# The first norm of a two-block network: TensorE computes the shifts, and products are interleaved with the normed tiles

## What is computed

```python
def modulate(h, shift, scale):
    return h * (1 + scale[:, None, :]) + shift[:, None, :]

def macaron_ffn(x, mod3, norm_pre, norm_post, w_gate, w_up, w_down):
    h = modulate(rms_norm(x, norm_pre), mod3[:, 0], mod3[:, 1])
    y = (jax.nn.silu(h @ w_gate) * (h @ w_up)) @ w_down
    return x + MACARON_WEIGHT * mod3[:, 2][:, None, :] * rms_norm(y, norm_post)

mod = (jax.nn.silu(c) @ ada_w[layer] + ada_b[layer]).reshape(b, N_MOD, D_MODEL)
mod_ctx = (jax.nn.silu(c_ctx) @ ada_w[layer] + ada_b[layer]).reshape(1, N_MOD, D_MODEL)
x = macaron_ffn(x, mod[:, 0:3], *ffn1)
ctx = macaron_ffn(ctx, mod_ctx[:, 0:3], *ffn1)
```

## Time and profile before

| | |
|---|---|
| median of three runs | 3566.09 us (3564.87 to 3566.77) |
| the profiled execution, its own time | 3565.38 us |
| its span, from first to last instruction | 3564.1 us |
| TensorE busy | 3456.8 us, 97% |
| VectorE, ScalarE, GpSimd busy | 46%, 40%, 34% |
| TensorE busy, 0 to 60 us | 31.2 us |
| granted TensorE clock, mean | 0.991 |
| chain that ended last | TensorE 87%, VectorE 6%, ScalarE 4% |

### The profile page before, as it was taken

The page is one execution under the profiler, slowest core; times in us unless marked ns, Lnnn a source line. Parts: engine busy times, 40 slices in busy tenths (PEclk is TensorE's granted clock), DMA queues, the critical chain, the costliest instruction groups (busy, mean ns, idle before and its releaser), DMA issues.

```text
span 3564.1 us, 44801 instructions
## 1 busy us (share of the span) xinstructions
PE 3456.8 (97%) x17264; PEld 2749.1 (77%) x17264; DVE 1653.8 (46%) x3091; ACT 1431.5 (40%) x2426; POOL 1225.3 (34%) x549
## 2 busy tenths in 40 slices
PE   6999999888999999999999999999999999999999
PEld 4888899776688887877776788887877776778887
DVE  7977466557420115655542333232855453234132
ACT  3223455554532223354443344343354453344242
POOL 2554200000044443434332444444434333334443
PEclk9999999999999999999999999999999999999999
DMA  8565365221123323222222222323322222223332
GB/s 316 192 225 192 125 189 165 71 84 54 48 89 89 101 89 103 84 71 89 83 77 82 84 89 92 99 92 110 100 76 84 78 74 89 83 83 97 98 94 85
DMA packets 118564, 376.42 MB, mean 106 GB/s; under 512 B 15440, under 2 KB 16336, under 8 KB 117968
## 3 DMA queue, kind: packets, MB, share of 16 engines
q1 hardware_dynamic: 115872, 367.88, 32.5%
q10 hardware_dynamic: 2480, 5.68, 0.5%
HBM read 359.86 MB, written 2.10 MB: 102 GB/s over the span
## 4 chain that ended last, share of the span: by engine, by line
PE 87%; DVE 6%; ACT 4%; issue 1%; DMA 1%; POOL 0%; SPq 0%; ACTq 0%; DVEq 0%; POOLq 0%
PE ps L1423 26%; PE ps L1425 25%; PE ps L1424 25%; PE ps L1683 2%; PE ps L1702 2%; ACT b L1765 1%; PE ps L1665 1%; PE ps L1466 1%; DVE b L2192 1%; PE ps L1661 1%; PE ps L1725 1%; PE ps L1736 1%; PE ps L1474 1%; DVE b L2355 1%; DVE b L2260 0%
## 5 line engine op out<-in xcount | busy, mean ns | idle before, releaser
L2682 POOL TENSOR_TENSOR b<-b,b 128x1024 fp32r<-128x1024 f32 (+1 forms) x501 | 1156.0, 2307 | 2268.9 <-ACT b L1765 2266.0
L1423 PE MATMUL ps<-b,b 128*128 128x512 f32 (+1 forms) x4720 | 1792.2, 380 | 48.2 <-DVE b L2192 15.4
L1425 PE MATMUL ps<-b,b 128*128 128x512 f32 (+1 forms) x4720 | 1754.0, 372 | 0.0
L1424 PE MATMUL ps<-b,b 128*128 128x512 f32 (+1 forms) x4720 | 1753.3, 371 | 0.0
L1423 PEld LDWEIGHTS ps<-b,b 128*128 128x128 f32 x4720 | 889.9, 189 | 278.0 <-issue 81.0
L1425 PEld LDWEIGHTS ps<-b,b 128*128 128x128 f32 x4720 | 890.2, 189 | 160.4
L1424 PEld LDWEIGHTS ps<-b,b 128*128 128x128 f32 x4720 | 891.0, 189 | 155.9 <-issue 5.8
L1765 ACT ACTIVATE b<-b 128x1024 fp32r<-128x1024 f32 (+2 forms) x622 | 607.1, 978 | 323.8 <-PE ps L1425 313.6
L2317 DVE CUSTOM_DVE_ANT_0 b<-b,b,b 128x1024 bf16<-128x1024 f32 x112 | 223.5, 1996 | 32.3 <-DMA b<-in_ada 21.4
L1826 ACT ACTIVATE b<-b 128x512 fp32r<-128x512 f32 (+1 forms) x110 | 64.8, 589 | 371.1 <-DVE b L2236 268.5
L2192 DVE TENSOR_TENSOR b<-b,b 128x1024 fp32r<-128x1024 f32 (+2 forms) x121 | 135.4, 1122 | 109.7 <-ACT b L1765 109.4
(11 more groups left out here) (236 smaller groups left out, 2406.6 us busy)
## 6 DMA issues: line engine op xcount, KB each, us to landing
b<-in_w SPq DMA_DIRECT2D x458, 512.0 KB, 3.5
b<-in_ada SPq DMA_DIRECT2D x88, 512.0 KB, 5.3
b<-in_w SPq DMA_DIRECT2D x80, 384.0 KB, 3.1
b<-in_w SPq DMA_DIRECT2D x80, 320.0 KB, 2.9
b<-b SPq DMA_DIRECT2D x176, 64.0 KB, 2.0
b<-in_const SPq DMA_DIRECT2D x24, 256.0 KB, 3.9
b<-in_x SPq DMA_DIRECT2D x2, 1024.0 KB, 12.0
out<-b SPq DMA_DIRECT2D x8, 256.0 KB, 2.0
```

Source lines behind the costliest of these rows:

```text
L1423: pe.matmul(out, a[0], b[0], start=first, stop=False)
L1424: pe.matmul(out, a[0], b[1], start=False, stop=False)
L1425: return pe.matmul(out, a[1], b[0], start=False, stop=last)
L2682: then(pool.tensor_tensor(wlo[j % NS][:, 0:nk * w], raw[j % NR][:, 0:nk * w], whi[j % NS][:, 0:nk * w].bitcast(F32), ALU.subtract), "lop", j)
```

## The change

- TensorE makes the eight shift tiles of the first norm: each by eight products of a 128x128 piece of `ada_w` with a two-column piece of the two vectors (c and c_ctx at once), and DVE adds the bias (a 128x2 instruction from PSUM, L2333 of the changed kernel). For these tiles the host lays `ada_w` out the other way round. The two vectors come in a small array of their own (`sc`, 128x16), silu on ACT.
- So DVE's `ada` instructions for these eight shifts go, and in ffn1 the eight for the context's shifts too: 96 such instructions stand where 112 did.
- The order of the head: the loads begin with `sc`, the first half of x, c, the second half; then w0, two modulation tiles, w1, two, w2, and the other twelve. The squares come first; `prime`, `factors(i)` (scale tile 2i, shift tile 2i+1, `gain1`), `pn` and the nine products with normed tile i-1 are written round by round. Six products that only keep TensorE at work stand behind the sum of squares.
- The last six triples of the three output tiles (k = 6 and 7) go tile by tile and no longer in turns.
- The second vector and modulation tiles 16 to 18 are loaded at `rest`, and the next weight chunks at the `prime` steps; the load of the context waits for the last shift tile.
- The weave's rate is 0.36 and its first steps are other ones.

```diff
-JOBS = ([(p, (0,)) for i in range(8) for p in (8 + i, i)] + [(p, (1,)) for p in range(16)] + [(p, (0, 1)) for p in range(16, 40)]
+JOBS = ([j for i in range(8) for j in ((8 + i, (0,)), (i, (0, 1)))] + [(p, (1,)) for p in range(8, 16)] + [(p, (0, 1)) for p in range(16, 40)]
         + [(p, (0,)) for p in range(40, 72)])
+BY_TENSOR = tuple(range(1, 16, 2))
...
-    S += [do("init")] + ada[:2] + squares(0) + ada[2:10] + [do("gain1", i=i) for i in range(5)] + norm[:1]
-    S += [do("sel"), do("prime", j=0)] + norm[1:3]
-    for i in range(3):
-        S += ada[10 + 2 * i:12 + 2 * i] + [do("gain1", i=5 + i)] + ([do("prime", j=1 + i)] if i < 2 else []) + norm[3 + i:4 + i]
-    S += norm[6:] + [do("rest"), do("silu2")]
-    S += weave(ffn(0, "ffn1", ("pn", 0), L, 2),
-               ada[16:32] + [do("gain", k=0)] + [x for a in ada[32:56] for x in (a, do("gap"))] + ada[56:]
-               + squares(1) + prenorm(1), 0.38)
+    def factors(i):
+        return ada[2 * i:2 * i + 2] + [do("gain1", i=i)]
+    main = weave(ffn(0, "ffn1", ("pn", 0), L, 2),
+                 [do("gap")] * 6 + ada[16:24] + [do("gain", k=0)] + [x for a in ada[24:48] for x in (a, do("gap"))] + ada[48:]
+                 + squares(1) + prenorm(1), 0.36)
+    done = max(i for i, s in enumerate(main) if s["kind"] == "mm" and s["t"]["i"] < 2 and s["t"]["name"] == "fg" and s["last"])
+    first, main = [s for s in main[:done + 1] if s["kind"] != "gap"], main[done + 1:]
+    end = [first[19 + x + 3 * y] for x in range(3) for y in range(2)]
+    S += [do("init")] + squares(0) + [do("prime", j=0)] + factors(0) + norm[:1] + idle(0, 6) + [do("sel")]
+    S += norm[1:2] + [do("prime", j=1)] + factors(1) + norm[2:3] + [do("prime", j=2)] + first[:4]
+    for i in range(2, 8):
+        S += factors(i) + norm[1 + i:2 + i] + (first[3 * i - 2:3 * i + 1] if i < 7 else [])
+    S += norm[9:] + [do("rest"), do("silu2")] + end + main
...
+            elif k == "ada" and st["x"] in BY_TENSOR:
+                x = st["x"]
+                at.wait_ge(*n("cb", 2))
+                at.wait_ge(*ada_sem(x))
+                b = bank_of(st["bank"])
+                for i in range(8):
+                    p = pe.matmul(b[:, 0:2], ada_slot(x)[:, 128 * i:128 * i + 128], sc[:, :, i], start=(i == 0), stop=(i == 7))
+                p.then_inc(up("pada", x), 1)
...
             elif k == "rest":
+                at.wait_ge(*n("ada", BY_TENSOR[-1]))
                 act.dma_start(CX[:, :, :], CT.rearrange("p (t n) -> p t n", t=8)).then_inc(s["d_cx"], 16)
...
+                if x in BY_TENSOR:
+                    at.wait_ge(*n("pada", x))
+                    dve.tensor_scalar(mod[:, p, :], PB[st["bank"]][:, 0:2], pv("ada_b", p), None, ALU.add).then_inc(
+                        up("ada", x), 1)
+                    continue
```

More of the change, by code:

```diff
@@ L382, in schedule @@
     norm = prenorm(0)
-    S += [do("init")] + ada[:2] + squares(0) + ada[2:10] + [do("gain1", i=i) for i in range(5)] + norm[:1]
-    S += [do("sel"), do("prime", j=0)] + norm[1:3]
-    for i in range(3):
-        S += ada[10 + 2 * i:12 + 2 * i] + [do("gain1", i=5 + i)] + ([do("prime", j=1 + i)] if i < 2 else []) + norm[3 + i:4 + i]
-    S += norm[6:] + [do("rest"), do("silu2")]
-    S += weave(ffn(0, "ffn1", ("pn", 0), L, 2),
-               ada[16:32] + [do("gain", k=0)] + [x for a in ada[32:56] for x in (a, do("gap"))] + ada[56:]
-               + squares(1) + prenorm(1), 0.38)
+    def factors(i):
[5 more added lines that the diff above has]
+    first, main = [s for s in main[:done + 1] if s["kind"] != "gap"], main[done + 1:]
+    assert len(first) == 25 and first[0]["kind"] == "begin" and all(s["kind"] == "mm" for s in first[1:])
+    end = [first[19 + x + 3 * y] for x in range(3) for y in range(2)]
[4 more added lines that the diff above has]
+    S += norm[9:] + [do("rest"), do("silu2")] + end + main
     S += [do("gain", k=k) for k in range(1, 8)]
@@ L685, in number @@
         if k == "init":
+            mark("cb", 2)
             mark("cb", 0)
@@ L790, in number @@
         elif k == "ada":
+            if s["x"] in BY_TENSOR:
+                s["bank"] = brief()
+                mark("pada", s["x"])
             mark("ada", s["x"])
@@ L1173, in program @@
              "d_blk", "d_strip", "d_dh0", "d_dh1", "d_dh2", "d_dh3", "d_out"] + [f"d_raw{i}" for i in range(NR)]
[L1174 removed]
+            + [f"d_ada{i}" for i in range(15)] + [f"d_ring{i}" for i in range(4)] + ["d_cb0", "d_cb1", "d_sc"])
     s = {k: ctx.enter_context(nc.semaphore(k)) for k in list(SIGNALS) + DMAS + ["dve_own"]}
@@ L1319, in sp_program @@
             if k == "init":
+                sp.dma_start(sc[:, :, :], CB[:, 2048:2064].rearrange("p (v k) -> p v k", v=2)).then_inc(s["d_sc"], 16)
+                xt_ = XT.rearrange("p (t n) -> p t n", t=8)
+                sp.dma_start(X[:, 0:4, :], xt_[:, 0:4, :]).then_inc(s["d_x0"], 16)
                 sp.dma_start(cb[:, 0, :], CB[:, 0:1024]).then_inc(s["d_cb0"], 16)
-                xt_ = XT.rearrange("p (t n) -> p t n", t=8)
-                for x in range(4):
-                    load_ada(x)
[L1324 to L1333, removed]
-                for x in range(12, 14):
-                    load_ada(x)
-                load(2)
-                for x in range(14, 16):
-                    load_ada(x)
+                sp.dma_start(X[:, 4:8, :], xt_[:, 4:8, :]).then_inc(s["d_x1"], 16)
+                load(0)
+                load_ada(0)
+                load_ada(1)
+                load(1)
+                load_ada(2)
+                load_ada(3)
+                load(2)
+                for x in range(4, 16):
+                    load_ada(x)
+            elif k == "prime":
+                load(NR + st["j"])
+            elif k == "rest":
                 sp.dma_start(cb[:, 1, :], CB[:, 1024:2048]).then_inc(s["d_cb1"], 16)
@@ L1341, in sp_program @@
                     load_ada(x)
-            elif k == "rest":
-                for c in range(NR, 2 * NR):
-                    load(c)
             elif k == "begin":
```

11 lines of the change are left out of this document (8 added, 3 removed).

## The result

The changed kernel takes 3591.97 us (median of 4 runs, 3589.97 to 3595.75) against 3565.48 us before (also 4 runs, 3560.38 to 3566.77): a ratio of 1.0078, 95% interval 1.0061 to 1.0096. The forecast was 3594.0 us, with a range of 3578 to 3602, and slower by more than 0.2%. The profiled execution took 3595.75 us (span 3594.4 us), against 3565.38 before, 30.4 us more.

What follows compares the result with a forecast made beforehand. The head was taken as bound by VectorE, with the change worth only what it moves TensorE's restart: 86.3 - 58.4 = +27.9 us. Added to the profiled 3565.4 that gives 3593.3, and 0.7 for the median 3594.0 us; range 3578 to 3602.

Steps and rivals of the forecast that it cites:

- the mark: Moment TensorE goes on behind the first three output tiles: 58.37 us before, forecast 86.3, +27.9 us.
- Part 1: Loads and sum of squares: first square at 10.7 us, last two passes at 21.6, a gain of 2 us.
- Part 2: Up to the first shared round: TensorE starts at 30.3 us, small products of i = 2 end at 35.9.
- Part 3: Price of a set of eight small products: 1.75 us at full clock, 3.5 at half.
- Part 4: Rounds i = 3 to 7: TensorE and VectorE take turns, 7.8 us a round, last small products end at 74.9.
- rival of full clock: Clock stays full in the rounds: 6.0 us each, +18.9 us, 3585 us; chance 0.22.
- Part 5: End of the head: three tiles end at 81.5 us, late second vector delays TensorE from 82.6 to 86.3.
- the third sign of being wrong: At the end of the head: the second vector is there before chunk 0 is done.
- All at half: Rival: rounds wholly at half clock, 9.5 us each, 3605 us; chance 0.12.
- No change: Rival: nearly free small products, vector landing in 3.5 us, VectorE's part 1.6: rounds of 4, +5 us, 3571; chance 0.05.
- Nearly free small products: Rival: small products cost almost nothing, rounds of 4.6 us, +10.5 us, 3576 us; chance 0.07.
- Faster: Rival: TensorE runs ahead of VectorE and loads decide; TensorE goes on at 47, -11 us, 3555; chance 0.04.

Runs made afterwards that it cites:

- e11_after: The changed kernel run and profiled once more, with nothing changed; 3592.44 us in one run.
- e1_ahead: The changed kernel with each set of small products one round earlier on TensorE, ahead of the nine products of the round; 3568.67 us.
- e5_fill: The changed kernel with six full-width products nobody reads between each set of small products and the nine that wait for VectorE; 3583.13 us.
- e3_early: The changed kernel with the second vector loaded right behind the sixteenth modulation tile; 3592.57 us in one run.
- e8_both: e1_ahead with the second vector loaded right behind the sixteenth modulation tile, as in e3_early; 3565.74 us.
- e4_one: The changed kernel with only the first of the eight small products in each set; 3572.35 us in one run.
- e9_hold: e8_both with eight products nobody reads in TensorE's wait ahead of the first nine products; 3561.83 us.
- e7_warm: The kernel before with its last six triples tile by tile and products nobody reads in TensorE's waits ahead of the first three triples; 3564.02 us.

## Why the prediction was right, point by point

**The bound and the mark.** That the change is worth what it moves the mark held: 28.97 of 30.4 us in the profiles, 26.5 between the medians. The prediction named as a sign of being wrong that the time behind the head differs by more than 2 us. It was 1.3 us longer in the first profile and 2.2 shorter in the second (e11_after), which no more than the spread between profiles explains here.

**Part 1.** First square at 10.66 (forecast 10.7), the last passes from 20.09, 1.10 long (21.6 forecast, 21.2 measured).

**Part 2.** TensorE starts at 29.39 (forecast 30.3), the first nine end at 33.4 (34.1), the set of i = 2 at 36.8 (35.9): this set was forecast at full clock and ran at half. The two errors cancel within 1 us.

**Part 3.** A set is 1.84 us at full and 3.41 at half clock (forecast 1.75 and 3.5). A pass is 0.115 us at full clock and 0.213 at half, and two columns cost no less than the twelve of the earlier trace rows (0.109). That it is the weight load which sets this is argued from the durations; no run changed the weights. The Trainium skill (TensorE: Matmul & The Clock Gate, section LDWEIGHTS) gives a weight load of 128 columns as 107 ns; the spacing of the passes comes near it at full clock and not at half, where it is 213 ns.

**Part 4.** Turn-taking, the decisive step, is shown by e1_ahead. VectorE's part leaves TensorE idle for 1.83 us, and 2.2 was forecast: the two waits of VectorE on its own semaphore were priced too high (bias and gain together took 0.33 us and not 0.6). The mixed clock (nine mostly at half, set at full) came in three rounds of five (7.60, 7.18 and 7.46 us); the other two were at half throughout, 9.25. So the term "7.8 a round" measured 8.15. The first shared set ended 0.9 late and the five rounds added 1.7, so the last set ends at 77.5 instead of 74.9, 2.6 late. VectorE was idle for 4.1 to 6.3 us in a round and not for some 3. The argument for the rival of full clock, that no wait of a round is as long as the 2.5 us seen before the fall at 59.95, failed: waits of 1.83 us went with half clock in some part of every round. The Trainium skill (TensorE: Matmul & The Clock Gate, section A second HAM failure mode: psum-queue depth-cycling) tells of a kernel in which short idle times between groups of products make the clock swing; e5_fill agrees, since the fill of the 1.83 us brought a steady clock.

**Part 5.** Here the sizes were off most, and in part cancelled. The 18 last products with VectorE's part were forecast at 6.6 us and took 7.5, the first six and part of the seventh at half clock, so the three tiles end at 85.1 and not at 81.5. But the mark hung on the second vector: issued at 78.18 (forecast 75.6, late with the rounds), there 4.6 later and not 5.9, silu at 82.76 (forecast 81.5). The split of chunk 3 started at 83.72 and the mark came 3.62 later (3.78). The late vector was said to cost 3.7 us (86.3 against 82.6); e3_early shows 1.3, since with the slower rounds and last products chunk 0 itself was done only at 82.1 and not at 78.8. The vector came 0.7 us behind it: it did hold the end, but the third sign of being wrong was close. ScalarE's table load (79.40, 1.28) was left out of the working; it lay in the wait for the vector and cost nothing here. In e3_early too ScalarE was idle behind silu, for 0.62 us, so it cost nothing there either. With the short rounds of e8_both it does cost a little: table load (56.40), silu and chunk 3's split (58.65) follow each other there without idle time, and chunk 0 was done at about 58.2.

**What was luck.** The mark was forecast at 86.3 and came at 87.34. The mechanism was right: the turns, the clock that is lost in them and the late vector. That the moment is met within 1.1 us is in part luck: the rounds and what led to them are 2.6 us late, and the load that landed 1.3 us sooner than its term, with shorter steps behind it, took back 1.6 of them. The clock was a choice of one pattern for all rounds, and it came in three of five; a round of 8.15 us lies between that pattern and the one at half throughout.

**The rivals.** Full clock: not held. All at half: two rounds of five. No change: the rounds of the changed kernel are all above 7 us. Nearly free small products: excluded by 1.84 us. Faster: it was to decide if the small products could pass the nine, and e1_ahead lets them. But that gives no gain: the rival's mark of 47 counted the loads as the bound and left out that each set takes 1.84 us of TensorE's own time, so that a round is 3.87 us even at full clock, longer than its two tiles take to land (1.24 us each).

## What to carry to other kernels

Work that is moved to an idle engine must also be placed ahead in that engine's queue: the same small products go with a head that is 29 us or 3 us longer, by standing behind or ahead of the products that use the result of the round before. Count a round as a cycle through both queues, and look for the instruction that waits for something that was written too late. Where an engine's clock falls when it waits, cover the waits and see whether the rounds get shorter although work was added (e5_fill). Then profile twice, and compare the profiled execution with the median, because the clock may come back at another moment in the next execution.

## What was not expected of the hardware

- TensorE 82% busy, with waits of 1.83 us and narrow products, got 1.2 GHz for whole rounds (granted clock 0.50 from 30 to 50 us). With the same waits and an eighth of the narrow products it did so too (e4_one, 0.52 from 50 to 60 us). The same nine and set without idle time held 2.4 GHz for over 20 us (e1_ahead, 34 to 57).
- Without any idle time from the first nine products on, e8_both stayed at half clock until about 41.5 us in one execution and about 49 in another, while e1_ahead, with the same order on TensorE, left it at 33.3.
- The clock fell while TensorE was busy without a break: with two-column products at 25.0 us in e9_hold, and in the middle of full-width products 1 us after an idle time of 2.61 us had ended (e7_warm, 40.4 to 43.7).
- A set of 16 passes of two columns takes 3.41 instead of 1.84 us at half clock, nearly the full factor of two, although it streams next to nothing.
